# Weight pieces of experts 4 to 26 asked for as two half DMAs, from SyncE's and from ScalarE's queue

## What is computed

```python
def moe_ffn(h, w_router, b_router, w_gu, b_gu, w_down, b_down):
    logits = (hf @ w_router + b_router).astype(f32)
    top_val, top_idx = lax.top_k(logits, TOP_K)      # 4 of 32
    gate = jax.nn.softmax(top_val, axis=-1)
    ...
    def expert_block(args):
        xb, e = args
        gu = xb @ w_gu[e] + b_gu[e]
        g, u = gu[:, :D_FF], gu[:, D_FF:]
        g = jnp.minimum(g, SWIGLU_LIMIT)
        u = jnp.clip(u, -SWIGLU_LIMIT, SWIGLU_LIMIT)
        return ((u + 1.0) * (g * jax.nn.sigmoid(SWIGLU_ALPHA * g))) @ w_down[e] + b_down[e]
```

## Time and profile before

| | us |
|---|---|
| median of 3 runs (1255.32 to 1258.51) | 1255.58 |
| the profiled execution | 1255.34 |
| its span on the core | 1253.6 |
| TensorE busy in the span | 1204.7 |
| ScalarE busy | 150.7 |
| VectorE busy | 402.0 |
| packets of queue q1, share of 16 DMA engines | 87.7% |
| median from request to landing, w_gu to ring, 60 DMAs | 28.2 |

### The profile page before, as it was taken

One profiled execution on the slowest core, in us unless ns is written; L12 is line 12 of the kernel. 1 busy time (PEld: TensorE's weight loads), 2 busy tenths in 40 slices (PEclk: granted clock), 3 DMA queues, 4 the chain that ended last, 5 costly groups with the idle time before them and its releaser, 6 DMA issues.

```text
span 1253.6 us, 16096 instructions
## 1 busy us (share of the span) xinstructions
PE 1204.7 (96%) x6673; PEld 608.7 (49%) x6673; DVE 402.0 (32%) x802; ACT 150.7 (12%) x345; POOL 8.0 (1%) x33
## 2 busy tenths in 40 slices
PE   9999999999999999999999999999999999999987
PEld 8999985768443334333333343333333344333322
DVE  5786766583731122111111122111112132111112
ACT  2234432014100000000000000000000000000002
POOL 1000000000000000000000000000000000000000
PEclk9999999999999999999999999999999999999999
DMA  9963223479589999999999999999999999999996
GB/s 296 357 221 134 114 90 144 176 267 352 217 314 427 427 428 428 427 428 430 428 428 428 429 428 428 428 428 430 428 428 428 429 428 427 428 427 428 428 426 273
DMA packets 61895, 454.76 MB, mean 363 GB/s; under 512 B 7388, under 2 KB 14232, under 8 KB 35224
## 3 DMA queue, kind: packets, MB, share of 16 engines
q1 hardware_dynamic: 59464, 452.23, 87.7%
q10 hardware_dynamic: 2384, 1.84, 0.5%
HBM read 453.00 MB, written 1.05 MB: 362 GB/s over the span
## 4 chain that ended last, share of the span: by engine, by line
PE 69%; DMA 29%; SPq 1%; issue 1%; DVE 0%; ACT 0%; DVEq 0%; ACTq 0%
PE ps L1606 32%; DMA r_odd<-in_w_gu_dram 18%; DMA ring<-in_w_down_dram 10%; PE ps L1269 6%; PE ps L1410 4%; PE ps L1581 3%; PE ps L1599 3%; PE ps L1062 2%; PE ps L1168 2%; PE ps L1471 2%; PE ps L1267 2%; PE ps L1557 2%; PE ps L1166 1%; PE ps L1716 1%; DMA ring<-in_w_in_dram 1%; PE ps L1711 1%
## 5 line engine op out<-in xcount | busy, mean ns | idle before, releaser
L1606 PE MATMUL ps<-ring,r_memT 128*64 128x512 f32 x1024 | 225.8, 594 | 13.3 <-DMA ring<-in_w_gu_dram 12.6
L1606 PE MATMUL ps<-r_odd,r_memT 128*64 128x512 f32 x1024 | 225.2, 594 | 13.1 <-DMA r_odd<-in_w_gu_dram 13.1
L2511 DVE TENSOR_SCALAR r_ga<-ps 128x512 f32<-128x512 f32 x32 | 22.1, 692 | 632.5 <-PE ps L1606 632.5
L1606 PE MATMUL ps<-ring,r_ga 128*64 128x512 f32 x760 | 173.1, 604 | 11.0 <-DMA ring<-in_w_down_dram 11.0
L1606 PEld LDWEIGHTS ps<-r_odd,r_memT 128*64 128x64 f32 x1024 | 72.0, 137 | 163.7 <-issue 136.0
L1606 PEld LDWEIGHTS ps<-ring,r_memT 128*64 128x64 f32 x1024 | 72.0, 137 | 160.7 <-issue 135.6
L1606 PEld LDWEIGHTS ps<-ring,r_ga 128*64 128x64 f32 x760 | 53.4, 139 | 127.5 <-issue 98.0
L992 ACT ACTIVATE r_ga<-r_ga 128x512 f32<-128x512 f32 x31 | 19.5, 630 | 508.4 <-PE ps L1599 489.6
L1581 PE MATMUL ps<-r_dm,r_x 128*128 128x128 f32 x512 | 65.7, 282 | 0.4 <-DVE r_dm L2432 0.4
L1599 PE MATMUL ps<-r_ga,r_dm 64*128 64x512 f32 x256 | 63.6, 615 | 0.7 <-ACT r_ga L1003 0.7
L1581 PEld LDWEIGHTS ps<-r_dm,r_x 128*128 128x128 f32 x512 | 62.8, 197 | 1.3 <-issue 1.3
(11 more groups left out here) (426 smaller groups left out, 1085.2 us busy)
## 6 DMA issues: line engine op xcount, KB each, us to landing
ring<-in_w_gu_dram SPq DMA_DIRECT2D x60, 2048.0 KB, 28.2
r_odd<-in_w_gu_dram SPq DMA_DIRECT2D x59, 2048.0 KB, 27.8
ring<-in_w_down_dram SPq DMA_DIRECT2D x43, 2048.0 KB, 22.6
r_gbx<-in_w_down_dram SPq DMA_DIRECT2D x14, 2048.0 KB, 32.5
ring<-in_w_in_dram SPq DMA_DIRECT2D x7, 2048.0 KB, 18.3
r_odd<-in_w_gu_dram SPq DMA_DIRECT2D x10, 1024.0 KB, 14.1
ring<-in_w_down_dram SPq DMA_DIRECT2D x9, 1024.0 KB, 7.8
ring<-in_w_gu_dram SPq DMA_DIRECT2D x8, 1024.0 KB, 7.7
```

What stands on the lines that cost most here:

```text
L1606: last = mm(ps[n * SLOTS:(n + 1) * SLOTS, bk, :], stationary_, moving(n), start=start, stop=stop, skip_group_check=True)
L2511: V.tensor_scalar(gact, ps[:, GBK, :], 7.0, None, ALU.min).then_inc(g_limited, 1)
```

## The change

For experts 4 to 26 (`SHARED`) SyncE asks only for partitions 0 to 63 of each piece (`parts = P // 2`). Partitions 64 to 127 are asked for by ScalarE, in `upper_piece`, with the same wait for the slot and with a 16 of its own on the slot's semaphore. ScalarE's requests stand in `block_steps`: in block i the upper halves of pieces 0 to 2 of expert i+2 ahead of the wait for `g_limited`; piece 3 behind the sigmoid; piece 4 behind the copy to `scat`; and `dn1` of expert i+1 behind the copy to `y_slot`. TensorE waits for counts that have 16 more for each shared use of a slot (`upper_count`, or its end value with `late`). Experts 0 to 3 and 27 to 31 stay as they were. The order of SyncE's requests is unchanged. The core of the diff:

```diff
+SHARED = range(4, 27)
...
-            def expert_piece(e, j):
+            def expert_piece(e, j, parts=P):
...
-                sp.dma_start(dst, src).then_inc(loaded[s], 16)
+                sp.dma_start(dst[0:parts], src[0:parts]).then_inc(loaded[s], 16)
...
-            def odd_heads(p, part=range(HEADS)):
+            def odd_heads(p, part=range(HEADS), parts=P // 2):
 
                 for j in part:
                     sp.wait_ge(odd_freed[j], p)
-                    odd_piece(p * 2 + 1, j)
+                    odd_piece(p * 2 + 1, j, parts)
...
-            others(2)
+            others(2, P)
             even_heads(2)
-            others(3)
+            others(3, P)
...
-            with sp.Fori(AHEAD + 3, NE // 2 - 1) as p:
+            last_shared = SHARED[-1] // 2
+            with sp.Fori(AHEAD + 3, last_shared) as p:
                 odd_heads(p)
                 others(p * 2 + 1)
                 even_heads(p + 1)
                 others(p * 2 + 2)
+            with sp.Fori(last_shared, NE // 2 - 1) as p:
+                odd_heads(p, parts=P)
+                others(p * 2 + 1, P)
+                even_heads(p + 1, parts=P)
+                others(p * 2 + 2, P)
...
+            def upper_piece(e, turn, j, odd):
+                if odd and j < HEADS:
+                    act.wait_ge(odd_freed[j], turn)
+                    dst, landed = odd_slot[j], odd_loaded[j]
+                else:
+                    s = eslot[EXPERT_PIECES[j]]
+                    act.wait_ge(freed[s], turn)
+                    dst, landed = ring[:, s].rearrange("p (k n) -> p k n", k=2 if j < 4 else 4), loaded[s]
+                src = gu_dram[e, j] if j < 4 else dn_dram[e, j - 4]
+                act.dma_start(dst[P // 2:P], src[P // 2:P]).then_inc(landed, 16)
...
+            def block_steps(i, last=False, turn=None, odd=False, last_piece=False):
+                if turn is not None:
+                    upper_heads(i + 2, turn, range(3), odd)
                 act.wait_ge(g_limited, i + 1)
...
                 nc.scalar.activation(sig_last if is_block(i, NE - 1) else sig, gact, ACT.Sigmoid, scale=1.702)\
                     .then_inc(sig_done, 1)
+                if turn is not None:
+                    upper_heads(i + 2, turn, range(3, 4), odd)
...
                 nc.scalar.activation(scat, ps[:, GBK, 0:T], ACT.Copy).then_inc(scat_ready, 1)
...
+                if turn is not None:
+                    upper_heads(i + 2, turn, range(4, HEADS), odd)
                 act.wait_ge(freed[eslot["dn1"]], i + 1)
                 nc.scalar.activation(y_slot, ps[:, ZBK, :], ACT.Copy).then_inc(yslot_ready, 1)
+                if last_piece:
+                    upper_piece(i + 1, i + 1, HEADS, False)
...
-            with act.Fori(1, NE - 1) as i:
+            block_steps(1)
+            block_steps(2, turn=2)
+            block_steps(3, turn=2, odd=True, last_piece=True)
+            with act.Fori(2, 12) as p:
+                block_steps(p * 2, turn=p + 1, last_piece=True)
+                block_steps(p * 2 + 1, turn=p + 1, odd=True, last_piece=True)
+            block_steps(24, turn=13, last_piece=True)
+            block_steps(25, last_piece=True)
+            with act.Fori(26, NE - 1) as i:
                 block_steps(i)
```

More of the change, by code:

```diff
@@ L609, in odd_half, with odd_piece, even_heads, others @@
                 sp.dma_start(odd_slot[j][:, k], gu_dram[e, j][:, k]).then_inc(odd_loaded[j], 16)
-            def odd_piece(e, j):
-                sp.dma_start(odd_slot[j], gu_dram[e, j] if j < 4 else dn_dram[e, j - 4]).then_inc(odd_loaded[j], 16)
-            def odd_heads(p, part=range(HEADS)):
+            def odd_piece(e, j, parts=P):
+                src = gu_dram[e, j] if j < 4 else dn_dram[e, j - 4]
+                sp.dma_start(odd_slot[j][0:parts], src[0:parts]).then_inc(odd_loaded[j], 16)
+            def odd_heads(p, part=range(HEADS), parts=P // 2):
                 for j in part:
                     sp.wait_ge(odd_freed[j], p)
-                    odd_piece(p * 2 + 1, j)
-            def even_heads(p, part=range(HEADS)):
+                    odd_piece(p * 2 + 1, j, parts)
+            def even_heads(p, part=range(HEADS), parts=P // 2):
                 for j in part:
                     sp.wait_ge(freed[eslot[EXPERT_PIECES[j]]], p)
-                    expert_piece(p * 2, j)
-            def others(i):
+                    expert_piece(p * 2, j, parts)
+            def others(i, parts=P // 2):
                 for j in range(HEADS, 6):
                     sp.wait_ge(freed[eslot[EXPERT_PIECES[j]]], i)
-                    expert_piece(i, j)
+                    expert_piece(i, j, parts)
             def heads(e, part):
@@ L987, in _, with upper_heads @@
             last.then_inc(r_exp, 1)
-            def block_steps(i, last=False):
+            def upper_piece(e, turn, j, odd):
[6 more added lines that the diff above has]
+                    dst, landed = ring[:, s].rearrange("p (k n) -> p k n", k=2 if j < 4 else 4), loaded[s]
+                src = gu_dram[e, j] if j < 4 else dn_dram[e, j - 4]
+                act.dma_start(dst[P // 2:P], src[P // 2:P]).then_inc(landed, 16)
+            def upper_heads(e, turn, part, odd):
+                for j in part:
+                    upper_piece(e, turn, j, odd)
+            def block_steps(i, last=False, turn=None, odd=False, last_piece=False):
+                if turn is not None:
+                    upper_heads(i + 2, turn, range(3), odd)
                 act.wait_ge(g_limited, i + 1)
@@ L1664, in second_half, with upper_count, piece_rows @@
                     pe.wait_ge(rest_loaded[j - 3], 16)
-            def piece_rows(j, uses, odd):
+            def upper_count(j, uses, odd):
+                first = SHARED[0] if j == HEADS else SHARED[0] // 2
+                last = SHARED[-1] if j == HEADS else (SHARED[-1] - odd) // 2
+                if isinstance(uses, int):
+                    return uses * 16 + 16 * (min(max(uses - first + 1, 0), last - first + 1))
+                return uses * 32 + 16 * (1 - first)
+            def piece_rows(j, uses, odd, late=False):
+                count = uses * 16 + 16 * ((SHARED[-1] if j == HEADS else SHARED[-1] // 2) - \
+                                          (SHARED[0] if j == HEADS else SHARED[0] // 2) + 1) \
+                    if late else upper_count(j, uses, odd)
                 if odd and j < HEADS:
-                    pe.wait_ge(odd_loaded[j], uses * 16 + (32 if j < 3 else 16))
+                    pe.wait_ge(odd_loaded[j], count + (32 if j < 3 else 16))
                     return lambda k, a: odd_slot[j][:, k, a:a + 512]
                 s = eslot[EXPERT_PIECES[j]]
-                pe.wait_ge(loaded[s], uses * 16 + (16 * dmas[s] + 16))
+                pe.wait_ge(loaded[s], count + (16 * dmas[s] + 16))
                 w = ring[:, s].rearrange("p (k n) -> p k n", k=2 if j < 4 else 4)
@@ L1679, in piece_rows, with gate_up @@
                 return lambda k, a: w[:, k, a:a + 512]
-            def gate_up(xs_, i, heads_used, odd, after):
+            def gate_up(xs_, i, heads_used, odd, after, late=False):
                 for j in range(4):
@@ L1692, in gate_up @@
                         pe.wait_ge(odd_first_loaded[0], 16)
-                    w = piece_rows(j, heads_used if j < HEADS else i, odd)
+                    w = piece_rows(j, heads_used if j < HEADS else i, odd, late)
                     for k in range(2):
@@ L1722, in turn_hidden_half, with down @@
                 last.then_inc(ht_done if half else ht_half, 1)
-            def down(i, heads_used, odd):
+            def down(i, heads_used, odd, late=False):
                 for j in range(2):
@@ L1729, in down @@
                         pe.wait_ge(odd_first_loaded[4], 16)
-                    w = piece_rows(4 + j, heads_used if 4 + j < HEADS else i, odd)
+                    w = piece_rows(4 + j, heads_used if 4 + j < HEADS else i, odd, late)
                     for k in range(4):
@@ L1809, in late_block @@
                 pe.wait_ge(xg_ready, i + 1)
-                gate_up(lambda kk: xg[:, 0, kk, 0:SLOTS], i, i - NE // 2, False, lambda j: None)
+                gate_up(lambda kk: xg[:, 0, kk, 0:SLOTS], i, i - NE // 2, False, lambda j: None, True)
                 pe.wait_ge(placeg_ready, i + 1)
@@ L1816, in late_block @@
                 pe.wait_ge(hT_ready, i + 1)
-                down(i, i - NE // 2, False)
+                down(i, i - NE // 2, False, True)
                 pe.wait_ge(yslot_ready, i + 1)
```

## The result

| | before | after |
|---|---|---|
| median, us | 1256.12 (1255.32 to 1258.51, 4 runs) | 1652.01 (1636.43 to 1682.28, 4 runs) |
| the profiled execution, us | 1255.34 | 1682.28 |
| its span, us | 1253.6 | 1680.5 |
| mean GB/s, 450 us to the end of the stretch in question | 428 | 267 |

The changed kernel takes 1.31 times as long (95% interval 1.3045 to 1.3156); by the medians of the table it is 396 us more.

What follows compares the result with a forecast made beforehand. The stream of weights through the DMA engines was taken to bound the kernel. 1255.3 us, plus 1.4 for completion packets and 24.5 for half pieces of lead, made 1281.2, forecast 1281 us; range 1247 to 1440 us.

Steps and rivals of the forecast that it cites:

- What bounds the kernel: Weight stream through the 16 DMA engines, without a gap at 428 GB/s: 29.4 us an expert against TensorE's 26.4 us.
- (a): Small completion packets on the stream: 138 more for each engine at 9.8 ns, +1.4 us.
- (b): ScalarE's queue: 138 more DMA issues of 0.5 us, 69 us in all, asked for in time or covered; cost 0.
- (c): SyncE and ScalarE ask for dn1 and the next heads in different orders after experts 12 to 16; cost 0, no slack.
- (d): Price of half pieces in the shared stream: each partition half limited to 214 GB/s, unequal streams lose time; +24.5 us.
- rival 4: Shared stream: paired engines stay in step, lower then upper half, so 289 MB go at 221 GB/s; 1888 us, chance 0.08.
- rival 3: Shared stream: engines collide all the time over the same half, packets 1.27 times as long; 1438 us, chance 0.22.
- A piece of lead: Upper halves running ahead beside whole pieces: 2.45 us lost at the entry, 2.45 at the exit, 4.9 us each half piece.
- The number of leads: Half pieces by which ScalarE's queue leads from the entry at 405 us: 5 taken, bounds 2 and 8.

Runs made afterwards that it cites:

- the transfers alone: Programs that only move expert weights, no layer computed; lower halves from SyncE beside upper halves from ScalarE made 223 GB/s, in a longer stage 225.
- the first program: Only transfers of expert weights, no layer computed, eleven stages each from an empty queue; whole pieces 418 GB/s from SyncE, 419 from both queues.
- SyncE's order alone: The changed kernel, but SyncE asks for both halves, upper right behind lower, and ScalarE for none: two runs, 1797.59 and 1904.13 us.
- a regular stream: Only transfers, no layer computed: 50 pieces as lower halves from SyncE and upper halves from ScalarE, ten slots; 225 GB/s for 450 us.
- fifth stage: Only transfers, no layer computed: lower halves from SyncE and upper halves from ScalarE at once, 16 KB packets; 223 GB/s.
- the repeated pattern: Only transfers: eight experts of five whole pieces and a lower half from SyncE, the upper half from ScalarE; 305 us for 100.7 MB.

## Why the prediction was wrong

**What bounds the kernel, and the rest of the frame: right.** The stream of weights set the time, before and after, and its rate accounts for 423 of 427 us.

**(a) Completion packets, +1.4 us: not contradicted.** The even and odd partitions have 138 more DMAs as well. Their profiled execution lies 6.7 us above the one before, of which 5.2 are the dip at the exit; the 1.5 left are near the term, but single executions of before differ by up to 3.5 us, so no run shows it.

**(b) and (c), ScalarE's issues and the two orders, 0: right.** Column halves from two queues and from one: 1269.47 and 1269.59 us.

**(d) The price of a half: the step that failed.** The first half of it held. That "one half of the partitions can be filled at some 214 GB/s at most, whoever asks", read from the 221 GB/s of the earlier trace rows, came out as 210 for lower halves alone. The next sentence, "Equal streams to both halves can still make 428", had no row behind it, and it is the step that failed. From it followed that only leads count, 4.9 us for each half piece of lead and 24.5 us in all. Measured, equal streams made 223 to 225 GB/s in the transfers alone and 267 in the kernel, so the price ran through all 289 MB.

The reason is in the prediction's own rival 4, which was held to be unlikely (0.08) since "q1 and q10 alternated without loss in the earlier trace rows". Those were DMAs of 128 partitions, and such DMAs lose nothing in the first program either: 418 from one queue, 419 from two. What hindered one another in the runs were DMAs of one half, and the row said nothing of those. Nor does it show the turns packet by packet that the lead was counted with: q1 moved 1447 packets there and q10 272. By the earlier trace rows, the only row in which a queue with part of the partitions ran beside one with all, packets grew 1.27 times; here they grew 1.54 times (0.95 over 0.615). There q10 asked for 0.23 MB beside 1.40, here for half of everything, which is a likely reason for the difference. The truth lies between rival 3's 1438 and rival 4's 1888.

**Why 1652 and not 1888.** SyncE's order alone comes near rival 4, 218 GB/s and 1798 to 1904 us. Two queues make 225 in a regular stream and 267 in the kernel. What follows is a picture that fits, argued and not shown. If two engines on one way start their packets a little apart, each packet has the way to itself for that little while, and they keep their distance: a packet takes 2 x 0.611 us less the distance. Medians over the packets of each stage (no view prints them) give 0.08 us of distance for the 1.14 us of a packet in the first program's fifth stage, and for runs of 8, 4 and 2 KB (0.536, 0.228 and 0.098 us beside 0.309, 0.159 and 0.084 in the kernel before) 0.08, 0.09 and 0.07: nearly one distance for four sizes. It doesn't fit everything: lower halves alone took 1.28 us a packet, more than twice 0.611. In the kernel, 0.95 us would be a distance of 0.27. That the kernel's irregular requests make it larger is argued; no run varied it.

**A piece of lead, 4.9 us: mis-sized too.** For one upper and one lower half among whole pieces the transfers alone gave 7 us, in the repeated pattern 8.8, and the kernel 10.8. The 1369 us that the arithmetic gave for dn1 alone were 1506. The number of leads had a weak source too: a landing 13.2 us after its request is 2.7 pieces of 4.9 us, the piece itself among them, and not the 2.3 pieces ahead of it that were counted.

**A reading.** The earlier trace rows show the DMA engines at 9 from the thirteenth slice on, not the twelfth, which has 8 and 314 GB/s. Nothing else hangs on it.

## What to carry to other kernels

In these runs a transfer at the full rate needed partitions from both sides of 64 in every DMA, and two DMAs side by side, one for each side, didn't make up for it. If a piece must be split between queues, split it by even and odd partitions (+3 us here) or by columns (+12 us here), never at partition 64 (+396 us). And when a sum rests on "these two together can still make the full rate", find a row that shows two such streams together, or give the case without it the same weight.

## What the runs showed of the hardware that was not expected

- 64 partitions are enough for nearly the full rate if they lie on both sides: 32 to 95 made 410 GB/s from one queue, even and odd ones from two queues 428 in the kernel; 0 to 63 made 210.
- Lower and upper halves at the same time from two queues: 223, 242, 275 and 328 GB/s with runs of 16, 8, 4 and 2 KB. Here alone shorter runs are faster.
- An upper and a lower half of 1 MB each, among whole pieces, held the stream at 215 GB/s for 16 us in the kernel with only dn1 shared. The 3.44 MB of that time would have taken 8 us at 428: whole pieces beside a half are slowed with it.
- Packets of 8 KB instead of 16 KB to all partitions cost 1.4% of the rate (422 against 428 GB/s).
